# Ten background steps for every pair of weight units in the mixer stage

## The reference, cut to what matters

```python
proj = u @ w_in[layer]
aq, ak, av, rq, rf, ri, rg, ga, gb = jnp.split(proj, splits, axis=-1)
att = sliding_window_attention(aq, ak, av, rel_bias, attn_sinks[layer])   # 8 query heads
rec = hgrn2_recurrence(rq, rf, ri, lower_bounds[layer])                  # 4 heads, 128 x 128 state
rec = rms_norm(rec, rec_norm[layer]) * jax.nn.sigmoid(rg)
y_a = att @ w_att_proj[layer]
y_b = rec @ w_rec_proj[layer]
merged = jax.nn.sigmoid(ga) * y_a + jax.nn.sigmoid(gb) * y_b
h = h + merged @ w_out[layer]
```

## Time and profile before

| | before |
|---|---|
| median of 3 runs | 1833.7 us (1830.22 to 1833.85) |
| profiled execution: its own time | 1827.06 us |
| profiled execution: span | 1825.3 us |
| mean granted TensorE clock | 0.982 |
| PE busy | 1729.6 us, 95% of the span |
| DVE busy | 1093.3 us, 60% |
| ACT busy | 882.1 us, 48% |
| share of PE on the chain that ended last | 70% |

### The profile page before, as it was taken

How to read it: one execution, slowest core, us unless ns; L and a number is a source line. 1 busy time by engine, 2 the same in 40 slices (tenths; PEclk the granted TensorE clock), 3 DMA queues, 4 the chain that set the end, 5 groups by cost and what they waited for, 6 DMA issues and landing times.

```text
span 1825.3 us, 28082 instructions
## 1 busy us (share of the span) xinstructions
PE 1729.6 (95%) x11935; PEld 1581.3 (87%) x11935; DVE 1093.3 (60%) x1411; ACT 882.1 (48%) x1370; POOL 165.9 (9%) x192
## 2 busy tenths in 40 slices
PE   7999999999998999998999998999999997999996
PEld 6899799899977998977789997899989887899995
DVE  5455567678765544667565555655566575655554
ACT  5344466544564455452454445544454444444443
POOL 0000001218001012800000000000000000000000
PEclk9999999999999999998999999999999998999998
DMA  6755534454544444531445554465544331455551
GB/s 225 236 186 187 179 139 142 168 189 178 190 156 166 172 169 142 184 113 47 175 154 185 185 187 159 164 220 185 185 154 181 119 113 70 159 205 185 185 185 69
DMA packets 51084, 300.97 MB, mean 165 GB/s; under 512 B 6072, under 2 KB 12688, under 8 KB 17168
## 3 DMA queue, kind: packets, MB, share of 16 engines
q1 hardware_dynamic: 50800, 298.66, 45.8%
q0 software_dynamic: 160, 0.52, 0.1%
HBM read 298.08 MB, written 1.09 MB: 164 GB/s over the span
## 4 chain that ended last, share of the span: by engine, by line
PE 70%; DVE 11%; ACT 10%; DMA 3%; issue 3%; POOL 1%; SPq 1%; DVEq 0%; ACTq 0%; POOLq 0%
PE PS L1793 67%; DVE wlo L1109 4%; ACT whi L634 3%; DMA raw<-in_w 3%; ACT wk L677 2%; PE PS L1796 1%; DVE xn L1194 1%; POOL st L526 1%; ACT SC L766 1%; PE PS L1913 1%; DVE SC L1347 1%; DVE X L1186 1%; ACT SC L854 1%; DVE SC L1503 0%; DMA SC<-in_pT 0%
## 5 line engine op out<-in xcount | busy, mean ns | idle before, releaser
L1109 DVE TENSOR_TENSOR wlo<-raw,whi 128x1024 fp32r<-128x1024 f32 x528 | 660.5, 1260 | 446.6 <-ACT whi L634 445.6
L634 ACT ACTIVATE whi<-raw 128x1024 fp32r<-128x1024 f32 x528 | 550.1, 1053 | 414.2 <-PE PS L1793 251.7
L1793 PE MATMUL PS<-xhi,whi 128*128 128x256 f32 x2536 | 724.9, 286 | 5.7 <-DVE wlo L1109 5.0
L1793 PE MATMUL PS<-xhi,wlo 128*128 128x256 f32 x2536 | 719.1, 284 | 0.0
L1793 PE MATMUL PS<-xlo,whi 128*128 128x256 f32 x2536 | 710.7, 284 | 0.0
L1793 PEld LDWEIGHTS PS<-xhi,whi 128*128 128x128 f32 x2536 | 489.5, 193 | 13.9 <-DVE wlo L1109 7.6
L1793 PEld LDWEIGHTS PS<-xhi,wlo 128*128 128x128 f32 x2536 | 489.6, 193 | 0.0
L1793 PEld LDWEIGHTS PS<-xlo,whi 128*128 128x128 f32 x2536 | 484.7, 193 | 2.0
L1793 PE MATMUL PS<-whi,hhi 128*128 128x512 f32 x544 | 170.3, 394 | 2.4 <-DVE wlo L1109 2.4
L1793 PE MATMUL PS<-wlo,hhi 128*128 128x512 f32 x544 | 168.9, 392 | 0.0
L1793 PE MATMUL PS<-whi,hlo 128*128 128x512 f32 x544 | 168.3, 391 | 0.0
(11 more groups left out here) (261 smaller groups left out, 1444.0 us busy)
## 6 DMA issues: line engine op xcount, KB each, us to landing
raw<-in_w SPq DMA_DIRECT2D x264, 1024.0 KB, 4.8
gr<-in_rows SPq DMA_DIRECT2D x23, 512.0 KB, 3.8
SC<-scratch SPq DMA_DIRECT2D x1, 2048.0 KB, 12.0
SC<-scratch SPq DMA_DIRECT2D x2, 1024.0 KB, 11.9
X<-in_x SPq DMA_DIRECT2D x2, 512.0 KB, 4.8
xn<-in_sc SPq DMA_DIRECT2D x2, 512.0 KB, 7.3
out<-xn SPq DMA_DIRECT2D x2, 512.0 KB, 2.7
SC<-in_pT SPq DMA_DIRECT2D x3, 256.0 KB, 4.0
```

Source lines behind the costliest of these rows:

```text
L634: a.activation(whi[:, u % NSPLIT, :], raw[:, u // 2 % NRAW, u % 2 * HU:u % 2 * HU + HU], ACT.Copy).then_inc(s_hi, 1)
L1109: v.tensor_tensor(wlo[:, u % NSPLIT, :], src, hi.bitcast(f32), SUB).then_inc(s_lo, 1)
L1793: return pe.matmul(o, l, r, start=start, stop=stop)
```

## The change

The four input gate half units get four background steps each (before two), and every pair gets five steps between its half units (before one), with one behind it and four after as before: ten for every pair. The same numbers are changed on all three engines. No instruction's work is changed; the background steps stand earlier, and the drain holds fewer of them.

```diff
@@ scalar, vector: mixers()
-                def pair():
-                    half_unit(v0[0])
+                def pair(n=1):
+                    half_unit(v0[0], n)
                     half_unit(v0[0] + 1)
                     v0[0] += 2
...
                 for c in range(4):
-                    half_unit(v0[0], 2)
+                    half_unit(v0[0], 4)
                     v0[0] += 1
...
                 for j in range(8):
...
                     if j in (4, 6):
-                        pair()
+                        pair(5)
                         bg.fill(4)
-                    pair()
+                    pair(5)
                     bg.fill(4)
@@ tensor: mixers()
                         half_unit(u0[0], PS[:, b, 0:S])
-                    bg.fill()
+                    bg.fill(n)
                     half_unit(u0[0] + 1, PS[:, b, S:2 * S])
                     bg.fill()
...
                     e.then_inc(s_used, 1)
-                    bg.fill(2)
+                    bg.fill(4)
```

More of the change, by code:

```diff
@@ L1043, in mixers @@
                     if j in (4, 6):
-                        q.wait_ge(s_used, pair())
+                        q.wait_ge(s_used, pair(5))
                         a.activation(sgr[:, j - 4:j - 2, :], two(4 + n % 2), ACT.Sigmoid).then_inc(m_rg, 1)
```

## The result

Over eleven timed runs of each, the changed kernel took 1838.25 us in the median (1828.83 to 1844.44), the kernel before 1829.74 us (1825.78 to 1833.85): a ratio of 1.0044, with a 95% interval of 1.0029 to 1.0060, some 8 us. The forecast was 2.4 us slower. Its time of 1836.1 us lies only 2.1 us under the measured one because it was counted from the first three runs of the kernel before, whose median (1833.7 us) is 4.0 us above that of all eleven.

What follows compares the result with a forecast made beforehand. PE, busy for 95% of the span, was taken as the bound. Removing 15.4 us and adding 13.9 of stalls and 3.9 of low clock gave +2.4 on 1833.7, so 1836.1 us, range 1828.5 to 1842.

Steps and rivals of the forecast that it cites:

- The likeliest forecast: Whole kernel: +2.4 us, taken with its neighbour as a change of -3.7 to +3.7 us; chance 0.50.
- rival 2: c2 to P6: clock falls behind each stall, five falls instead of three, +5.0 us, about 1840; chance 0.36 with undervalued stalls.
- the wide range: Whole kernel: the range given, 1828.5 to 1842 us, leaving out the full rival of hidden steps and more than seven falls.
- The drain: After the last half unit: 21.5 us shrink to 6.0 plus 0.1 for hand-overs, removing 15.4 us there.
- the first scaling has no wait: In the drain: DVE's first scaling, 1.13 us, starts without waiting because the norm was ready long ago.
- The stalls: PE waits: 5.7 us at c2, 2.2 P0 to P1, 2.7 P2 to P4, 3.3 at P6, together 13.9.
- The table load: On ACT: 1.28 us, hidden at c2 but on the path before the fourth exponentials at P6.
- The clock: Behind the three stalls over 2 us: PE's clock falls, 1.3 us each, 3.9 us together.
- The sum: Whole kernel: -15.4 us removed and 17.8 us of cost give +2.4 us, predicted time 1836.1 us.

Runs made afterwards that it cites:

- e5: Changed kernel, but at c1 ACT rounds P0b before the background steps, ahead of the first exponentials; stretch 172.54 us, 1.0004 of the kernel before.
- e8: Changed kernel plus matmuls nobody reads, filling all PE waits over 1 us; stretch 171.44 us, 0.9982 of the kernel before.
- e3: Changed kernel plus 38 matmuls nobody reads, filling most of PE's wait behind c2; stretch 177.05 us, 1.0027 of the kernel before.
- e10: e6 with three steps in the middle of P5 and four in P6, P7 and P8; stretch 167.45 us, 0.9959 of the kernel before.
- e6: e1 with the edit of e5 (P0b rounded before the background steps); stretch 166.96 us, 0.9966 of the kernel before.
- e1: Changed kernel with its four steps per input gate half unit, but pairs back at one middle step; stretch 171.10 us, 0.9990 of the kernel before.
- e9: e6 with three steps in the middle of P6, P7, P8 and P9; stretch 169.96 us, 0.9978 of the kernel before.

## Why the prediction was right in its direction and low in its size

The likeliest forecast was a change of at most 3.7 us to either side, with its own range of 1830 to 1837.4 us. The change was some 8 us and the time 1838.25 us, so it did not come true; what came is rival 2 (0.36, together with all else over +3.7), inside the wide range.

**The drain, right but for 0.9 us.** Forecast 6.1 us from the last half unit to the first `xhi` matmul, measured 7.0. The sentence that failed is "the first scaling has no wait, since the norm was ready long ago". The chain that ended last, in the drain:

```profile
1537.10 1.07 ACT whi L634
...
1538.20 0.07 DVE wlo L1109
...
1539.34 1.13 DVE xn L1642 x4
```

The norm was ready, but DVE's scaling (L1642) stands behind a `wlo`, whose rounding on ACT waited for PE to release a buffer. That is 0.64 us; the rest is the gate at 0.75 instead of 0.66, twice, and the transposes at 0.67.

**The stalls, right.** Behind c2 5.24 against 5.7, at s = 6 1.88 against 2.2, in P2 to P4 3.19 (1.62, 0.42 and 1.15) against 2.7, at P6 3.58 against 3.3: together 13.89 against 13.9. That the sum agrees to 0.01 us is luck: the single places are off by up to 0.5 us either way. The reason given for the first (the rounding of P0b behind the exponentials) is shown by e5. That the others are DVE's and ACT's lateness is what the waits name; no run took one of them away alone.

**The table load, right.** It lies on the path at P6, as forecast:

```profile
1510.21 1.28 ACT L986
...
1511.51 0.21 ACT st L986
```

The load takes 1.28 us and the next instruction starts within 0.02 us of its end. The 1.4 us more that the Trainium skill would add (ScalarE: Activation LUTs, What ACT_TABLE_LOAD costs: a drain behind the load) do not show here; the measurement decides for the sum without them.

**The clock, wrong in size.** The step was "I take the same 1.3 us behind the three stalls over 2 us: 3.9 us". There were five falls, at 1.5, 1.5, 1.5, 2.6 and 1.1 us: 8.1 us, shown by e8 for this profile. It failed twice. First, the rule "over 2 us": behind 1.62 and 1.15 us the clock fell as well, and at 1.88 us it did not; e3 shows the fall moving from one of these waits to the other, and e10 against e6 that the same instructions run with a fall and without. Second, the price of one: 1.3 us was read where 24 matmuls followed at the lower clock, while the fall behind P6 has 6.9 us at that level (twice 0.43 of 8.00 us, in the stretches above), against about 3.4 us in each of the others (the row of c2 begins behind the start of its fall). Rival 2 ("The clock stays low", five falls instead of three) is what happened in this profile. It gave P0 to P4 as their place; of the five, one lies behind c2, one at P6 and one at the first `xhi` matmul. At 1.3 us each it gave +5.0 for the whole change.

**The sum.** Forecast -15.4 + 13.9 + 3.9 = +2.4. Measured: +7.28 in the stretch. The clock makes 4.2 us of the difference (8.1 less 3.9). Without the clock the forecast was -15.4 + 13.9 = -1.5 and e8 shows -0.8, another 0.7, about the tail's 0.9. The two make the 4.9 us. A reading was off as well, and too small to matter: the moved transposes were taken at 0.65 us, where the earlier trace rows has 0.81, 0.3 us for the two sets. The median of the timed runs was 8.5 us above that of before (the ratio 1.0044 says 8), 0.8 to 1.2 us over the stretch.

**What stays open.** What decides whether a wait of 1 to 3 us brings a fall of the clock. The runs show that the length of the wait alone does not, and that the instructions around it do not either (e6 and e10). How many falls the changed kernel has in a typical execution is not known: each kernel was profiled once. The timed ratios of the changed kernel and e8 say only that filling the waits is worth 11.3 us, give or take some 4.

## What to carry to other kernels

Moving waiting from one long idle stretch into many short ones inside dense TensorE work can cost more than the waiting itself: here the changed kernel with its long waits filled came out even with the kernel before, and the falls of the clock behind the waits (8.1 us in the profile) were as large as the whole loss. Before steps of a background are brought forward, look at each in-order engine for what is queued behind the step; here one rounding placed ahead of the exponentials took 2.6 us off a wait, and with the falls that did not come 7.0 us off the stretch (4.1 us between e1 and e6). Matmuls that nobody reads, put in front of a wait, are a cheap way to measure what the clock costs in a kernel. Look at several executions before counting falls.

## What the runs showed of the hardware that I had not expected

The clock fell from 2.4 to 1.2 GHz behind a wait as short as 1.15 us, and stayed low with PE busy without a gap (PEclk 0.72 over the 6.00 us from 1489.87). Behind the same wait of 2.60 us in the same instructions it fell in e10 and not in e5, e6 and e9. Five falls, 20.4 us at the lower level, cost 8.1 us of 179.6. The kernel before has 20.5 us at the lower level, mostly in a drain with a half idle PE; what they cost it no run shows (the prediction put its one fall in dense work at 1.3 us). With waits of at most 0.74 us in the stretch, e8 held 1.00 all through it; over 180 us PE was busy for 173.79:

```profile
1410.00:1590.00 180.00, 173.79 (x1533) 155.86 (x1533) 115.81 (x191) 80.25 (x148) 3.56 (x6) 1.00 0.34 121
```
